# Attention units woven between a mixer's projections, their outputs in a place of their own, the rotary key as one product

## The reference

```python
for l in range(DEPTH):
    h = rmsnorm(x, norm1_g[l]) * (1.0 + sc1) + sh1
    x = x + g1 * hybrid_mixer(h, ...)
    h = rmsnorm(x, norm2_g[l]) * (1.0 + sc2) + sh2
    x = x + g2 * peer_ffn(h, ...)
```

```python
proj = h @ w_in            # split into the columns of four groups
y_a = dsa_attention(...)   # an indexer picks 64 keys of each query, then attention with a bias
y_b = mla_attention(...)   # queries and keys from small normalised latents, one shared rotary key
y_c = forgetting_attention(...)  # dense causal attention, a cumulative log gate added to the logits
y_d = s5_layer(...)        # a complex diagonal scan over time, then gelu and a gate
groups = rmsnorm(stack([y_a, y_b, y_c, y_d]), group_norm_g)
return groups.reshape(B, S, MIX_WIDTH) @ w_out
```

## Time and profile before

| | |
|---|---|
| median of 3 runs | 2326.34 us |
| lowest, highest | 2325.06, 2331.91 us |
| the profiled execution | 2331.42 us |
| its span in the profile | 2329.6 us |
| PE, DVE, ACT, POOL busy | 94%, 66%, 53%, 19% of the span |

### The profile page before, as it was taken

The page is one execution under the profiler, slowest core; times in us unless marked ns, Lnnn a source line. Parts: engine busy times, 40 slices in busy tenths (PEclk is TensorE's granted clock), DMA queues, the critical chain, the costliest instruction groups (busy, mean ns, idle before and its releaser), DMA issues.

```text
span 2329.6 us, 39958 instructions
## 1 busy us (share of the span) xinstructions
PE 2185.0 (94%) x13764; PEld 1979.4 (85%) x13764; DVE 1546.3 (66%) x3026; ACT 1229.7 (53%) x2330; POOL 439.3 (19%) x184
## 2 busy tenths in 40 slices
PE   5799799999999999999999979999999999999998
PEld 4687678999999988888878767899999998888886
DVE  7578436993478867777767843699347886555555
ACT  8622424455688854444442242445568885454553
POOL 0000016889300000000000001688930000000000
PEclk9799789999999999999999978999999999999999
DMA  7732034455444447777763203445544443555553
GB/s 263 258 102 98 28 129 136 154 180 172 139 142 144 138 151 257 265 261 261 264 226 110 91 28 109 136 154 180 171 142 139 144 138 126 195 190 195 192 191 106
DMA packets 103476, 378.81 MB, mean 163 GB/s; under 512 B 11488, under 2 KB 11872, under 8 KB 102880
## 3 DMA queue, kind: packets, MB, share of 16 engines
q1 hardware_dynamic: 102672, 373.74, 47.5%
q10 hardware_dynamic: 720, 4.00, 0.4%
HBM read 375.46 MB, written 2.23 MB: 162 GB/s over the span
## 4 chain that ended last, share of the span: by engine, by line
PE 74%; DVE 9%; issue 6%; POOL 5%; ACT 4%; DMA 2%; SPq 0%; POOLq 0%; ACTq 0%; DVEq 0%
PE bank L1633 30%; PE bank L1536 9%; PE bank L1537 9%; PE bank L1538 9%; POOL split_lo L478 5%; PE bank L1600 5%; PE bank L1324 3%; PE bank L1524 3%; DMA ring<-stream 2%; PE bank L1286 1%; ACT split_hi L671 1%; PE bank L1498 1%; DVE grid L841 1%; PE bank L1349 1%; PE bank L1297 1%
## 5 line engine op out<-in xcount | busy, mean ns | idle before, releaser
L1536 PE MATMUL bank<-h_hi,split_hi 128*128 128x256 f32 x2304 | 669.4, 291 | 25.7 <-POOL split_lo L478 11.2
L1537 PE MATMUL bank<-h_lo,split_hi 128*128 128x256 f32 x2304 | 654.5, 284 | 0.0
L1538 PE MATMUL bank<-h_hi,split_lo 128*128 128x256 f32 x2304 | 654.3, 284 | 0.0
L1536 PEld LDWEIGHTS bank<-h_hi,split_hi 128*128 128x128 f32 x2304 | 444.3, 193 | 32.8 <-POOL split_lo L478 16.9
L1184 DVE TENSOR_TENSOR split_lo<-ring,split_hi 128x1024 fp32r<-128x1024 f32 x248 | 303.8, 1225 | 252.6 <-ACT w_hi L759 252.5
L478 POOL TENSOR_TENSOR split_lo<-ring,split_hi 128x1024 fp32r<-128x1024 f32 x168 | 432.5, 2597 | 187.3 <-ACT split_hi L671 187.1
L758 ACT ACTIVATE split_hi<-ring 128x1024 fp32r<-128x1024 f32 x248 | 263.2, 1061 | 358.9 <-PE bank L1633 358.9
L1537 PEld LDWEIGHTS bank<-h_lo,split_hi 128*128 128x128 f32 x2304 | 445.1, 193 | 0.0
L1538 PEld LDWEIGHTS bank<-h_hi,split_lo 128*128 128x128 f32 x2304 | 444.3, 193 | 0.0
L671 ACT ACTIVATE split_hi<-ring 128x1024 fp32r<-128x1024 f32 x296 | 298.7, 1051 | 211.9 <-PE bank L1538 211.8
L1633 PE MATMUL bank<-split_hi,w_hi 128*128 128x512 f32 x1024 | 316.7, 390 | 0.0
(11 more groups left out here) (276 smaller groups left out, 2615.1 us busy)
## 6 DMA issues: line engine op xcount, KB each, us to landing
ring<-stream SPq DMA_DIRECT2D x658, 512.0 KB, 3.3
ada_ring<-stream SPq DMA_DIRECT2D x48, 512.0 KB, 4.3
spill<-tables ACTq DMA_DIRECT2D x1, 1152.0 KB, 4.2
tables<-spill ACTq DMA_DIRECT2D x1, 1152.0 KB, 7.3
xT<-x_in SPq DMA_DIRECT2D x1, 1024.0 KB, 9.8
s5raw<-s5w ACTq DMA_DIRECT2D x2, 512.0 KB, 6.0
y_out<-hT SPq DMA_DIRECT2D x1, 1024.0 KB, 3.9
KM<-mixc SPq DMA_DIRECT2D x1, 576.0 KB, 7.9
```

The lines of the kernel that those rows point to most:

```text
L1536: mm(dst, hi, x_hi, start=start, stop=False, skip_group_check=not group)
L1537: mm(dst, hi, x_lo, start=False, stop=False, skip_group_check=not group)
L1538: return mm(dst, lo, x_hi, start=False, stop=stop, skip_group_check=not group)
```

## The change

- PE's instructions of the mixer are cut into small functions and called in another order. The forgetting unit 0 has its logits after `fv0` and `fcum`, unit 1 after `cq1`; the sparse group now comes second (units 2, 3) and the latent group last (units 4, 5). `weighted` is split into `turned_probs` and `weighted`.
- The order of `MIX_BLOCKS` and of `REGIONS` follows, and so does ACT's order, which has exponents and copies of probabilities between the copies of projections.
- DVE's order is new too: the gate's inputs, the scans and the rounds of the indexer alternate, and the masks and maxima stand between the parts of the S5 turn-back.
- The first sine waits only for du0's copy.
- `ynT` has its own memory (72 to 80 KB of the slab), and so has `nlogf` (64 to 68 KB); the wait for fv1 ahead of the first write of `ynT` is gone.
- The rotary key is one `transposed("kr")` of 128 rows in place of two products of 64, and ACT copies its lower half into krA and its upper into krB.
- The first block of the output projection starts with the 12 records of the rows 6, 7, 4, 5, 0, 1 and needs unit 5 only for the last 4; the turn of unit 5 stands between them.

Buffers, and ACT's order at its beginning and its end:

```diff
-MIX_BLOCKS = ["du0", "du1", "B0", "iq0", "iq1", "ik", "aq0", "aq1", "ak0", "ak1", "B1", "av0", "av1",
-              "cq0", "cq1", "ckv", "kr", "fq0", "fq1", "fk0", "fk1", "fv0", "fv1", "UQ", "UKV"]
+MIX_BLOCKS = ["du0", "du1", "aq0", "B0", "ik", "iq0", "B1", "iq1", "fq0", "fk0", "fk1", "fq1", "fv0", "fv1",
+              "ckv", "cq0", "aq1", "cq1", "ak0", "av0", "av1", "ak1", "kr", "UQ", "UKV"]
...
-        ynT = hT
+        ynT = at_byte("ynT", 72 * KB, [KT, T])
...
-        nlogf = g(8192, TT, HEADS, P)
+        nlogf = at_byte("nlogf", 64 * KB, [TT, HEADS, P])
...
-            kt0 = [4, 2, 0][grp]
-            if n == 0:
-
-                act.wait_ge(region_filled, l * N_REG + REG_POS["fv1"] + 1)
+            kt0 = [4, 0, 2][grp]
...
+                copy(l, "du0", du[:, 0, :])
+                act.wait_ge(trig_arg, l + 1)
+                nc.scalar.activation(sinT, phase, ACT.Sin, scale=TWOPI).then_inc(trig_ready, 1)
+                copy(l, "du1", du[:, 1, :])
+                act.wait_ge(trig_arg2, l + 1)
+                nc.scalar.activation(cosT, tmp, ACT.Sin, scale=-TWOPI).then_inc(trig_ready, 1)
+                copy(l, "aq0", aq[:, 0, :], HD ** -0.5)
+                act.wait_ge(s5_lr, l + 1)
+                nc.scalar.activation(mag5, lr5, ACT.Exp).then_inc(s5_mag, 1)
+                copy(l, "iwcf", grid[:, 5632:5648])
+                copy(l, "ik", ik)
+                copy(l, "iq0", iq[:, 0, :])
+                copy(l, "iq1", iq[:, 1, :])
...
+                copy(l, "cq1", cq[:, 1, :])
+                copy(l, "ak0", ak[:, 0, :])
+                rows("av0", av, 0)
+                rows("av1", av, 1)
+                turned_copies(0)
+                act.wait_ge(act_taken, taken_count(l, "cq1")[1])
+                nc.scalar.activation(sqB[:, 0:2, :], cq, ACT.Square)
+                nc.scalar.activation(sqB[:, 2, :], ckv, ACT.Square).then_inc(sqB_ready, 1)
...
+                    nc.scalar.activation(kB[0:NOPE, h, :], take(l, f"kB{h}")[0:NOPE], ACT.Copy).then_inc(act_taken, 1)
+                turned_copies(3)
+                out_rows(act, l, 0, take)
+                for i in range(TT):
+                    copy(l, f"vB{i}", vB[:, i, :])
+                exponents(4)
+                for i in range(2):
+                    act.wait_ge(dve_taken, taken_count(l, f"y5_{i}")[1])
+                    nc.scalar.activation(g5[:, i, :], y5[:, i, :], ACT.Gelu_apprx_tanh).then_inc(g5_ready, 1)
+                turned_copies(4)
+                out_rows(act, l, 1, take)
+                out_rows(act, l, 2, take)
+                for i in range(2):
+                    nc.scalar.activation(sg5[:, i, :], take(l, f"glu{i}"), ACT.Sigmoid, bias=small_of(l, "bglu")[:, i:i + 1])\
+                        .then_inc(act_taken, 1)
+                exponents(5)
+                root(l, "ss5", GW, rstd)
+                turned_copies(5)
+                for n in range(3, 6):
+                    out_rows(act, l, n, take)
```

DVE's order up to the latents, and behind them:

```diff
+                dve.wait_ge(trig_ready, 2 * (l + 1))
+                turned_real(0)
+                forget_inputs()
+                turned_imaginary(0)
+                coefficients()
+                turned_real(1)
+                turned_imaginary(1)
+                scan(0)
+                scored(0)
+                forget_logs()
+                masked(0)
+                scan(1)
+                scored(1)
+                scan(2)
+                forget_mask(0)
+                scan(3)
+                forget_mask(1)
+                v.tensor_tensor(vim, cosT, zim, ALU.mult)
+                maxima(0)
+                link(v.tensor_tensor(turned_sin, sinT, zre, ALU.mult))
+                masked(1)
+                link(v.tensor_tensor(vre, cosT, zre, ALU.mult))
+                maxima(1)
+                v.tensor_tensor(vim, vim, turned_sin, ALU.add).then_inc(im_ready, 1)
+                link(v.tensor_tensor(phase, sinT, zim, ALU.mult))
+                outputs(0)
...
+                v.scalar_tensor_tensor(ckvn, ckv, sm("kvg")[:, 0:1], rstdB[:, 1, :], ALU.mult, ALU.mult)\
+                    .then_inc(latent_ready, 1)
+                outputs(1)
+                maxima(3)
+
+                dve.wait_ge(act_taken, taken_count(l, "kr")[1])
+                dve.wait_ge(im_ready, l + 1)
+                v.tensor_tensor(krA[hi], krA[hi], rope[hi, 1, :], ALU.mult)
+                link(v.tensor_tensor(krB[hi], krB[hi], rope[hi, 2, :], ALU.mult))
```

PE's order:

```diff
+                for n in ("du0", "du1", "aq0"):
+                    transposed(n)
+                s5_inputs(0)
+                index_weights()
+                transposed("ik")
+                transposed("iq0")
+                s5_inputs(1)
+                for n in ("iq1", "fq0", "fk0"):
+                    transposed(n)
+                index_dots()
+                for n in ("fk1", "fq1"):
+                    transposed(n)
+                by_rows("fv0")
+                forget_sums()
+                logits(0)
+                by_rows("fv1")
+                forget_columns()
+                for n in ("ckv", "cq0", "aq1", "cq1"):
+                    transposed(n)
+                logits(1)
+                transposed("ak0")
+                by_rows("av0")
+                turned_probs(0)
+                by_rows("av1")
+                transposed("ak1")
+                weighted(0)
+                latent_sums()
+                logits(2)
+                turned_probs(1)
+                transposed("kr")
+                weighted(1)
+                logits(3)
+                turned_probs(2)
+                latent_queries()
+                wkv = latent_keys()
+                weighted(2)
+                turned_probs(3)
+                turn(0)
+                logits(4)
+                latent_values(wkv)
+                s5_outputs()
+                weighted(3)
+                turn(1)
+                turn(2)
+                turned_probs(4)
+                logits(5)
+                s5_gates()
+                weighted(4)
+                pe.wait_ge(sq5_ready, l + 1)
+                sums_of(l, "ss5", sg5, 2)
+                turned_probs(5)
+                turn(3)
+                turn(4)
+                weighted(5)
+
+                order = (6, 7, 4, 5, 0, 1, 2, 3)
                 for m in range(KT):
                     b = load()
-                    r = free_region(l, f"out{m}")
-                    for k in range(KT):
-                        last = mm(r, b[:, k, :], ynT[:, k, :], start=(k == 0), stop=(k == KT - 1))
-                        if k == 0:
+                    if m == 0:
+                        pe.wait_ge(s5_out, l + 1)
+                        pe.wait_ge(act_taken, taken_count(l, "yt4")[1])
+                        r = region(l * N_REG + REG_POS["out0"])
+                    else:
+                        r = free_region(l, f"out{m}")
+                    for j, k in enumerate(order):
+                        if m == 0 and j == 6:
+                            turn(5)
+                            pe.wait_ge(act_taken, taken_count(l, "yt5")[1])
+                        last = mm(r, b[:, k, :], ynT[:, k, :], start=(j == 0), stop=(j == KT - 1))
+                        if j == 0:
                             free_block(last)
                     last.then_inc(region_filled, 1)
                     to_free[0] += 1
```

517 lines of the change are left out of this document (244 added, 273 removed).

## The result

The changed kernel took 2253.95 us (median of 4 runs, 2250.97 to 2255.97) for 2326.13 before: ratio 0.9684, 95% interval 0.9672 to 0.9697. The direction and the bound, PE's own work, held; the gain was 72 us for the forecast's 54.

A forecast was written before the change was run, and what follows sets the result against it. PE's own work was taken as the bound: 132.1 + 7.6 + 29.2 = 168.9 us per mixer at full clock, with two table loads 63.3 saved, less 9.6 for the clock, rounded 54: median 2272 us, range 2256 to 2298.

The forecast's parts named there:

- DVE's lead at unit 0: At unit 0's output, DVE gets there at 214 to 219 us and PE at 222, so DVE is 3 to 8 us ahead.
- The units' 25 us: Attention units of layer 0: PE's 33.6 busy us, mostly at 1.2 GHz, are 24.7 us of full-speed work, taken as 25.
- The clock's 4.8 us: End of each mixer: two spells at the lower clock of 2.4 us each, 9.6 us in all for both mixers.
- Waits: PE's idle time left per mixer: 2.4 in the projections, 3.2 at latent and S5 hand-offs, 2 at the end, together 7.6 us.
- The two table loads, 2.6 us: Root behind the output projection: no table load ahead of it any more, minus 1.3 us per layer on the path.
- The key: Rotary key in the projections: one product of 128 rows takes 3.5 us for 7.1 as two, minus 3.6.
- the columns: Forget columns, now behind fv1 with no wait ahead of them: 3.6 us for 5.4, minus 1.8.
- the output projection: End of the mixer: 28 us for eight projections plus 1.2 that stick out of unit 5's end, 29.2 for 30.7.
- the early sine: Start of the mixer: first sine waits only for du0's copy and DVE's phase, so DVE goes on 11 us earlier.
- The queues: Block fetches through the ring: slots come free in time as before, costed at nothing.
- Full clock with tight hand-offs (2261): Rival, chance 0.14: clock never falls at the mixer's end, 63.3 us come nearly whole and 2 us less idle, 2261.
- The lower clock for the whole end: Rival, chance 0.14: all from the latent queries on at 1.2 GHz, 12 to 13 us per mixer for 4.8, 2288.

## Why the prediction was right, and where it was wrong

**PE stays the bound: right.** PE is busy 96% of the stretch, a product more costs its full time, and DVE's lead at unit 0, forecast as 3 to 8 us, is 3.5.

**The sum: right in its terms, wrong in two sizes and one term.** For layer 0 the forecast was 132.1 of work, 4.8 of clock, 7.6 of waits and 29.2 of output projection, 173.7; measured are 127.6 (work and clock), 5.0 and 28.9, together 161.5. The stretch, forecast at 140 to 147 us, was 132.6 and 132.7.

- *The units' 25 us.* This is the step that failed first: "33.6 x (0.22 + 0.78 x 0.66)". Added up from the timeline, each group of records from its start to the next one's, the six units' logits, turned probabilities, values and turns take 20.4 us in layer 1, all at full clock: 4.6 less. (In layer 0 they take 21.4, with 1.0 of half clock at the end.) The row that I took for the full clock lay between the levels. With 2.00 / 3.67 = 0.54 the step gives 33.6 x (0.22 + 0.42) = 21.5; the last 1.1 us I did not resolve (the mean clock of 0.61 counts PE's waits too).
- *The clock's 4.8 us.* This term failed as well. The 94.5 us of the projections, which I took for work at full clock, already held a spell behind the index weights (these 4.47 and three projections 11.60, the dots between them 3.09, for 3.63, 10.63 and 1.68: 3.2 us). With the two new ones I charged 8.0 per mixer; layer 0 of the changed kernel pays 1.7 behind the index weights (8.84 for 7.17), 1.4 at the queries and 1.0 at the end. That is some 4 us less. Whether the spell at the queries comes differs between mixers with the same wait, and why stays open.
- *Waits.* 5.0 us in layer 0 and 5.9 in layer 1 for 7.6. The S5 hand-offs are covered by the units' records, as was meant; the end waits 1.38 and 0.64 for S5's squares and unit 5's exponents.
- *The two table loads, 2.6 us.* Wrong in its mechanism, and shown so: the root was not on the way. Output projection to first expert product went from 12.59 to 12.44 us. The third subtraction of POOL was on the way, in both kernels.

The mixers came out 12.2 and 12.1 us below the forecast. In layer 0 the units are 4.6 of that, the clock 3.9, the waits 2.6 and the output projection 0.3; 0.8 stays unassigned. The roots gave 2.3 us less than forecast. Together this is 22 of the 23 us by which the profiled execution, 2254.05, lay below the 2277 that I gave for it. The median of before is 5.1 us below its profiled execution and that of the changed kernel is not, so at the medians 18 are left.

**The other steps.** The key (3.62 for 3.5), the columns (3.62) and the output projection (28.9 for 29.2) held. DVE goes on 14.8 us behind the first projection, as forecast (143.9 - 129.1); but that the early sine is a gain by itself was not so: alone it cost time, and with the two S5 blocks moved, which I didn't count as a part, it paid. The queues cost nothing: no wait of a mixer names `ring`.

**The rivals.** Full clock with tight hand-offs (2261) was the nearest, and still 7 us too high: the clock did fall, but the work was less. The lower clock for the whole end did not come: 0.89 from the queries on.

## What to carry to other kernels

Where a wait precedes short products, price them from a row that lies wholly at the full clock, with the granted clock of its own window beside it; in the old units here, filling the waits with idle products, and nothing else, gave 17 us. A part that frees time in front of a wait can make a kernel slower, as the longer wait costs the clock behind it: judge such parts with the order that uses them, not alone. Before a saved load or root is counted, look at what the other engines do at the same moment: here a POOL subtraction held up a DVE product of two SBUF operands until it was over, 2.56 us for 0.41, and no releaser in the profile names it. And before a clock gain is read from one trace, look at the same place in other traces: here it came and went without an edit.

## What the runs showed of the hardware that was not expected

- A wait's length shows in the records behind it: the forget columns took 3.70 us behind 1.65 us of waiting, 5.39 behind 3.15 and 6.57 behind 10.17.
- Spells of half clock come where PE doesn't wait: behind the 32 index-weight products of 8 columns in 20 of 22 mixers of the changed kernel and its variants (8.84 for 7.17 in most), and once at the head of an output projection whose waits were filled (4.51 for 2.83).
- Behind the same wait of 1.98 us the same 16 products took 4.34 us in six mixers and 5.6 to 5.9 in five; only the execution differed, or parts of the kernel elsewhere.
- The same DVE subtraction of 128 x 256 takes 0.43 us, and 2.45 where it starts beside a POOL subtraction of 128 x 1024; a product that was stretched likewise made a table load of 1.28 us ahead of the root worth nothing.
